# A two-layer transformer kernel on one core: the small transfers leave GpSimd's queue for SyncE's and ScalarE's

## The reference, cut to what matters

```
layer 1: h = rmsnorm(x);  z = h @ w_in           (pooling, q, k, v, and an index head that picks 64 keys)
         x = x + concat(pool_mixer(..), attention(..)) @ w_out
         x = x + conv_ffn(rmsnorm(x))            (w_up 2048 x 11264, causal 3-tap conv, silu(gate)*val, w_down)
layer 2: proj = rmsnorm(x) @ w_in_2              (rope attention "moba", latent attention "mla", two gates)
         mixed = g_a * (y_a @ w_branch_a) + g_b * (y_b @ w_branch_b)
         x = x + mixed @ w_out_2
         x = x + (silu(hn @ w_gate) * (hn @ w_up)) @ w_down,  hn = rmsnorm(x);  out = rmsnorm(x)
```

## Time and profile before

| | us |
|---|---|
| median of 3 runs | 2383.08 |
| the profiled execution, its time | 2383.49 |
| the profiled execution, its span | 2381.6 |
| PE busy in the span | 2365.1 |
| DVE busy | 1390.7 |
| ACT busy | 1194.4 |
| POOL busy | 128.8 |

### The profile page before, as it was taken

The page is one execution under the profiler, slowest core; times in us unless marked ns, Lnnn a source line. Parts: engine busy times, 40 slices in busy tenths (PEclk is TensorE's granted clock), DMA queues, the critical chain, the costliest instruction groups (busy, mean ns, idle before and its releaser), DMA issues.

```text
span 2381.6 us, 29812 instructions
## 1 busy us (share of the span) xinstructions
PE 2365.1 (99%) x10624; PEld 1958.6 (82%) x10624; DVE 1390.7 (58%) x1574; ACT 1194.4 (50%) x1489; POOL 128.8 (5%) x228
## 2 busy tenths in 40 slices
PE   9999999999999999999999999999999999999997
PEld 7788888888888888888888888888888888888886
DVE  6785465776766765555554554766555555555543
ACT  6455455666666544445455544555444444444442
POOL 0100010000000000002130000122000000000000
PEclk9999999999999999999999999999999999999999
DMA  8775467788787766666776556666777777776554
GB/s 303 194 206 173 146 224 211 217 225 216 205 226 219 207 215 202 203 203 195 202 193 198 162 164 186 210 219 215 211 201 200 210 202 210 202 200 221 194 194 136
DMA packets 443082, 483.52 MB, mean 203 GB/s; under 512 B 208000, under 2 KB 225808, under 8 KB 442864
## 3 DMA queue, kind: packets, MB, share of 16 engines
q1 hardware_dynamic: 437712, 474.83, 67.7%
q0 software_dynamic: 4704, 6.44, 1.0%
q10 hardware_dynamic: 576, 1.05, 0.1%
HBM read 448.12 MB, written 2.10 MB: 189 GB/s over the span
## 4 chain that ended last, share of the span: by engine, by line
PE 97%; SPq 1%; issue 0%; DMA 0%; ACT 0%; DVE 0%; POOLq 0%; POOL 0%; DVEq 0%; ACTq 0%
PE acc L727 31%; PE acc L729 31%; PE acc L728 31%; SPq L504 1%; PE pair_banks L898 1%; PE bank L718 0%; PE pair_banks L929 0%; PE acc L753 0%; PE acc L757 0%; PE acc L760 0%; DMA w_raw<-in_w_in 0%; PE pair_banks L959 0%; PE pair_banks L870 0%; PE pair_banks L930 0%; SPq L373 0%
## 5 line engine op out<-in xcount | busy, mean ns | idle before, releaser
L1430 DVE TENSOR_TENSOR w_lo<-w_raw,w_hi 128x1024 fp32r<-128x1024 f32 (+1 forms) x842 | 1024.7, 1220 | 928.3 <-ACT w_hi L1068 926.7
L1068 ACT ACTIVATE w_hi<-w_raw 128x1024 fp32r<-128x1024 f32 (+1 forms) x842 | 886.2, 1055 | 1051.4 <-PE acc L729 1003.3
L727 PE MATMUL acc<-w_hi,xT 128*128 128x512 f32 (+1 forms) x2208 | 862.7, 391 | 0.0
L729 PE MATMUL acc<-w_hi,xT 128*128 128x512 f32 (+1 forms) x2208 | 857.1, 388 | 0.0
L728 PE MATMUL acc<-w_lo,xT 128*128 128x512 f32 (+1 forms) x2208 | 856.6, 388 | 0.0
L727 PEld LDWEIGHTS acc<-w_hi,xT 128*128 128x128 f32 x2208 | 414.6, 188 | 86.9 <-issue 2.3
L729 PEld LDWEIGHTS acc<-w_hi,xT 128*128 128x128 f32 x2208 | 414.5, 188 | 85.7
L728 PEld LDWEIGHTS acc<-w_lo,xT 128*128 128x128 f32 x2208 | 414.7, 188 | 83.5
L727 PE MATMUL acc<-w_hi,f_hi 128*128 128x512 f32 x688 | 267.6, 389 | 0.0
L728 PE MATMUL acc<-w_lo,f_hi 128*128 128x512 f32 x688 | 267.6, 389 | 0.0
L729 PE MATMUL acc<-w_hi,f_lo 128*128 128x512 f32 x688 | 267.6, 389 | 0.0
(11 more groups left out here) (220 smaller groups left out, 1308.4 us busy)
## 6 DMA issues: line engine op xcount, KB each, us to landing
w_raw<-in_w_up SPq DMA_DIRECT2D x264, 512.0 KB, 4.2
w_raw<-in_w_in SPq DMA_DIRECT2D x198, 512.0 KB, 3.8
w_raw<-in_w_down SPq DMA_DIRECT2D x176, 512.0 KB, 4.6
w_raw<-in_w_gate SPq DMA_DIRECT2D x88, 512.0 KB, 3.6
w_raw<-in_w_out SPq DMA_DIRECT2D x64, 512.0 KB, 4.6
w_raw<-in_w_branch_a SPq DMA_DIRECT2D x16, 512.0 KB, 4.2
w_raw<-in_w_branch_b SPq DMA_DIRECT2D x16, 512.0 KB, 4.8
halves<-stage SPq DMA_DIRECT2D x208, 32.0 KB, 2.6
```

The costliest lines, as they stand in the source:

```text
L727: pe.matmul(o, l, w_hi[:, slot, k, 0:width], start=start, stop=False)
L729: last = pe.matmul(o, m, w_hi[:, slot, k, 0:width], start=False, stop=stop)
L1068: act.activation(in_slot(w_hi, slot, width), in_slot(w_raw, slot, width), ACT.Copy).then_inc(w_split_hi, 1)
L1430: dve.tensor_tensor(in_slot(w_lo, slot, width), in_slot(w_raw, slot, width), in_slot(w_hi, slot, width).bitcast(F32), ALU.subtract).then_i ...
```

## The change

POOL issues no transfers. For n = 0, 1 and 2 of the residual groups and of the mix, SP issues all 16 transfers, four at each of the steps b to b+3, and the split (`split_x`, `split_mix`) moves from step b+3 to b+7. For n = 3 SP issues eight at step b as before and ScalarE the other eight at step b, and the split stays at b+3. The five loads of constants are issued by SP after the loads of chunks 19 to 23, that of pool_w by SP at its own step. The move steps of the units qn 1, qr and qa 1 come 2, 4 and 4 steps later, and `copy_k` of ka 2 steps later.

```diff
         put(n + lead, "blocks", u, g)
+        later = {("qn", 1): 2, ("qr", 2): 4, ("qa", 1): 4}.get((name, half), 0)
         for b in range(4):
-            put(n + lead + b, "move", u, g, b)
+            put(n + lead + later + b, "move", u, g, b)
         if name in ("k1", "ka"):
-            put(n + lead + 6, "copy_k", u, g)
+            put(n + lead + (6 if name == "k1" else 8), "copy_k", u, g)
...
-            put(b, "move_x", 0)
-            put(b, "move_x", 1)
-            put(b + 3, "split_x", n, gain)
+            for part in range(4) if n < 3 else (None,):
+                put(b + (part or 0), "move_x", n + 4 * quarters, part)
+            put(b + (7 if n < 3 else 3), "split_x", n, gain)
...
+    put(b + 19, "load_pool")
...
-        put(b, "move_mix", 0); put(b, "move_mix", 1); put(b + 3, "split_mix", n)
+        for part in range(4) if n < 3 else (None,):
+            put(b + (part or 0), "move_mix", n, part)
+        put(b + (7 if n < 3 else 3), "split_mix", n)
...
+        def move_blocks_of(queue, part, first_half, to, from_, done):
+
+            for k in range(4) if part is not None else range(8):
+                b, a_ = (part, k) if part is not None else (k // 2, k % 2 + (0 if first_half else 2))
+                move_block(queue, to, from_, b, a_).then_inc(done, 16)
+
+        def move_x(queue, n, part, first_half):
+
+            queue.wait_ge(x_blocks, NT * (n + 1))
+            move_blocks_of(queue, part, first_half, flat_stage[1], flat_stage[0], x_moved)
...
                 if not chunk.per:
+                    if 20 <= chunk.now < 25:
+                        load_constant(chunk.now - 20)
...
+                        elif step_ == "load_pool":
+
+                            sp.wait_ge(rel_full, 6)
+                            sp.dma_start(pool_w[:], a["pool_w"].rearrange("w (k p) d -> p w k d", p=P)).then_inc(pool_loaded, 16)
...
-            def on_move_x(half):
-                if half == 1:
-                    move_x(pool, x_moves, 1)
...
+            def on_move_x(n, part):
+                if part is None:
+                    move_x(act, n, part, False)
+
+            def on_move_mix(n, part):
+                if part is None:
+                    move_mix(act, n, part, False)
+
             def on_split_x(n, gain):
                 n_x[0] += 1
-                for half in range(2):
-                    act.wait_ge(x_moved[half], 16 * 8 * n_x[0])
+                act.wait_ge(x_moved, 256 * n_x[0])
```

More of the change, by code:

```diff
@@ L104, in attend, with residual @@
         put(a + 7, "split_y", which, pair)
-    def residual(n, g, b, gain):
+    def residual(n, g, b, gain, quarters=None):
         put(b, "res", g, n)
@@ L146, in plan @@
         b = group("w_out", CW * n, CW, [0, 1, 4, 5, 6, 7, 2, 3] if n == 0 else whole, "y")
-        residual(n, len(groups) - 1, b, G_FFN1)
+        residual(n, len(groups) - 1, b, G_FFN1, 0)
     up1 = b
@@ L154, in plan @@
         b = group("w_down", CW * n, CW, list(range(FT // KC)), "f")
-        residual(n, len(groups) - 1, b, G_ATTN2)
+        residual(n, len(groups) - 1, b, G_ATTN2, 1)
     b = group("w_in_2", 3072, 512, whole, "x")
@@ L191, in plan @@
         put(b, "mix_b", n, len(groups) - 1)
-        put(b, "move_mix", 0); put(b, "move_mix", 1); put(b + 3, "split_mix", n)
+        for part in range(4) if n < 3 else (None,):
+            put(b + (part or 0), "move_mix", n, part)
+        put(b + (7 if n < 3 else 3), "split_mix", n)
     for n in range(4):
         b = group("w_out_2", CW * n, CW, whole, "m")
-        residual(n, len(groups) - 1, b, G_FFN2)
+        residual(n, len(groups) - 1, b, G_FFN2, 2)
     up2 = b
@@ L356, in two_layer_kernel @@
         unit_blocks, unit_moved, k_copied = sem("unit_blocks"), [sem(f"unit_moved{k}") for k in range(4)], sem("k_copied")
-        mix_blocks, mix_moved = sem("mix_blocks"), [sem("mix_moved_sp"), sem("mix_moved_pool")]
+        mix_blocks, mix_moved = sem("mix_blocks"), sem("mix_moved")
         mix_high, mix_low = sem("mix_high"), sem("mix_low")
         x_blocks, x_high, x_low = sem("x_blocks"), sem("x_high"), sem("x_low")
-        x_moved = [sem("x_moved_sp"), sem("x_moved_pool")]
+        x_moved = sem("x_moved")
         dve_step, pool_step, normalised = sem("dve_step"), sem("pool_step"), sem("normalised")
@@ L373, in move_block, with move_mix @@
             return queue.dma_start(dst, src)
[L375 to L389, removed]
+        def move_blocks_of(queue, part, first_half, to, from_, done):
[5 more added lines that the diff above has]
+            move_blocks_of(queue, part, first_half, flat_stage[1], flat_stage[0], x_moved)
+        def move_mix(queue, n, part, first_half):
+            queue.wait_ge(mix_blocks, n + 1)
+            move_blocks_of(queue, part, first_half, flat_half, flat_stage[1], mix_moved)
         def turned(unit, q):
@@ L453, in _ @@
         def _(sp):
-            chunk, products, x_moves, mix_moves = Count(), Count(), [0, 0], [0, 0]
+            chunk, products = Count(), Count()
             def load_x(n):
@@ L482, in load, with load_constant @@
                 if not chunk.per:
+                    if 20 <= chunk.now < 25:
+                        load_constant(chunk.now - 20)
                     for step_, *args in at.get(chunk.now - RING - LEAD - 1, []):
[L484 to L487, removed]
+                        if step_ == "move_x":
+                            move_x(sp, *args, True)
+                        elif step_ == "move_mix":
+                            move_mix(sp, *args, True)
+                        elif step_ == "load_pool":
+                            sp.wait_ge(rel_full, 6)
+                            sp.dma_start(pool_w[:], a["pool_w"].rearrange("w (k p) d -> p w k d", p=P)).then_inc(pool_loaded, 16)
                         elif step_ == "move":
                             move_unit(*args)
+            def load_constant(k):
+                if k == 0:
+                    sp.dma_start(cols[:, CONV_COL:], a["columns"][:, CONV_COL:]).then_inc(taps_loaded, 16)
+                elif k == 1:
+                    sp.dma_start(causal[:], a["c_causal"]).then_inc(const_loaded, 16)
+                elif k == 2:
+                    sp.dma_start(pool_m[:], a["c_pool"]).then_inc(const_loaded, 16)
+                elif k == 3:
+                    sp.dma_start(cos[:, 0, :], a["c_freq"]).then_inc(const_loaded, 16)
+                else:
+                    sp.dma_start(pos_i[:], a["positions_2"][0, :].rearrange("(t p) -> p t", p=P),
+                                 allow_slow_non_contiguous=True).then_inc(const_loaded, 16)
             def move_unit(u, g, b):
@@ L594, in _ @@
         def _(pool):
[L597 to L607, removed]
+            n_rstd, n_heads, n_roped, n_lat, steps = [0], [0], [0], [0], [0]
             def step(ins):
@@ L627, in on_rstd @@
                 n_rstd[0] += 1
-                if n_rstd[0] == 1:
-                    load_constants()
-            def on_move_x(half):
-                if half == 1:
-                    move_x(pool, x_moves, 1)
-            def on_move_mix(half):
-                if half == 1:
-                    move_mix(pool, mix_moves, 1)
             def on_lat(kind):
@@ L683, in on_rope @@
                 pool.sem_inc(roped, 1)
-            mine = {"headsq": on_heads, "rstd": on_rstd, "rstd0": on_rstd, "lat_rstd": on_lat, "rope": on_rope,
-                    "move_x": on_move_x, "move_mix": on_move_mix}
+            mine = {"headsq": on_heads, "rstd": on_rstd, "rstd0": on_rstd, "lat_rstd": on_lat, "rope": on_rope}
             for n in range(n_end + 8):
                 for step_, *args in at.get(n, []):
-                    if step_ == "isc" and args[0] == 5:
-                        pool.wait_ge(rel_full, 6)
-                        pool.dma_start(pool_w[:], a["pool_w"].rearrange("w (k p) d -> p w k d", p=P)).then_inc(pool_loaded, 16)
                     if step_ in mine:
@@ L1218, in on_split_mix @@
             def on_split_mix(n):
-                for half in range(2):
-                    act.wait_ge(mix_moved[half], 16 * 8 * (n + 1))
+                act.wait_ge(mix_moved, 256 * (n + 1))
                 for q in range(4):
@@ L1266, in _ @@
                     "copy_p": on_copy_p, "copy_d": on_copy_d, "copy_kr": on_copy_kr, "copy_kn": on_copy_kn,
-                    "split_y": on_split_y, "split_x": on_split_x, "split_pool": on_split_pool,
+                    "split_y": on_split_y, "split_x": on_split_x, "move_x": on_move_x, "move_mix": on_move_mix, "split_pool": on_split_pool,
                     "split_lat": on_split_lat, "split_mix": on_split_mix, "square": on_square,
```

## The result

The changed kernel takes 2393.68 us (median of 5 runs, 2392.98 to 2395.88) against 2383.08 us before (2382.54 to 2383.52): slower by 10.6 us, a ratio of 1.0048 (95% interval 1.0035 to 1.0060). I had forecast 2383.8 and a range of 2378 to 2391.

The account below looks back on a forecast made before the run. TensorE was taken as busy nearly throughout, leaving the hole near 1184 to 1216 us, the tail and the group boundaries. -5.4 - 2.1 + 4.55 + 3.7 = +0.75 on 2383.08 gave 2383.8 us, range 2378 to 2391.

Parts of the forecast that it names:

- part 5: SP's added issues for n = 0 to 2 and the constants: delay hidden by ScalarE's three-chunk lead, cost nothing.
- part 4: ScalarE's eight issues for n = 3, 5.1 us a burst, make chunk b+4 late at four places: 3.7 us lost.
- the sum: Whole kernel: -5.4 - 2.1 + 4.55 + 3.7 = +0.75 us, no change that can be told.
- Part 1: Program's end: with no transfers issued by POOL its DRAIN is short, so the span ends 5.4 us earlier.
- Part 2: TensorE's three waits near 1184 to 1216 us: spreading the transfers and moving copy_k gains 2.1 us.
- Part 3: Split of n = 2 at b+7: stops before the next matrix, 1.6 (w_out), 1.6 (w_out_2), 1.35 (mix); 4.55 us.
- My sign of being wrong: ScalarE's row of eight issues for n = 3: under 4 or over 6 us would show the prediction wrong.
- rival B: ScalarE's n = 3 issues cost more beside SP's, sharing one generator; decides from 6.1 us a burst, 2404 at 10.2; chance 0.17.
- A: Program's end: POOL's DRAIN stays long, since powers also ran between the two DRAINs; +6.15, 2389.2 us, slower; chance 0.18.
- C: ScalarE's burst for n = 3 is cheap, 3.5 us like its own loads; sum -2.9, 2380.2 us; chance 0.17.
- D: Neither the b+7 split nor ScalarE's issues cost, the step order being misjudged; -7.5, 2375.6 us, faster; chance 0.1.
- E: Hole near 1184 to 1216 us: five issues in 3.2 us still lag, 2.1 not gained; 2385.9 us; chance 0.08.

Follow-up runs that it names:

- experiment 10: The kernel before, only with the later move steps of qn 1, qr and qa 1 and the later copy_k of ka: 2380.43 us, ratio 0.9989.
- experiment 9: The kernel before, only with the splits of n = 0 to 2 of x and mix at b+7: 2388.01 us, ratio 1.0020.
- experiment 7: The changed kernel with the splits of n = 0 to 2 at b+6 instead of b+7: 2398.28 us, ratio 1.0065.
- experiment 1: The changed kernel with POOL instead of ScalarE issuing the second eight transfers for n = 3: 2386.15 us, ratio 1.0014.
- experiment 8: The changed kernel with the mix as before (eight each on SP and POOL at step b, split at b+3): 2385.10 us, ratio 1.0011.
- experiment 5: The changed kernel with POOL taking SP's eight transfers for n = 3, ScalarE still issuing its eight: 2391.75 us, ratio 1.0037.
- experiment 6: The changed kernel with the 16 transfers of n = 3 dealt 12 to SP and 4 to ScalarE: 2387.18 us, ratio 1.0017.
- experiment 3: The changed kernel with one transfer, the load of pool_w, back on POOL: 2396.33 us, ratio 1.0055.
- experiment 4: The changed kernel with the move steps of qn 1, qr, qa 1 and copy_k where they were before: 2397.35 us, ratio 1.0060.

## Why the prediction was wrong

Three steps failed: part 5, which put SP's delay at nothing, for the mix (3.4 us of stop); part 4, whose burst of 5.1 us measured 5.42 to 6.92 (2.5 us); and the sum, which has no term for matmuls at half pace behind a stop (4.8 us).

**Part 1, the tail: right in size (5.4), incomplete in cause.** I took the DRAIN for a matter of yes or no. The experiments give 0.644 us with no transfer of POOL, 0.752 with 1, 3.287 with 32, 5.247 with 56, 5.898 with 64 and 11.125 with 134: 0.64 and 0.08 for each. It is their number, and not what they move: one load of 1 MB adds 0.108 us, 32 transfers that move 1 MB together add 2.64. So POOL could have kept about 60 for nothing, and the change paid to move these as well.

**Part 2, the hole: right.** 2.1 forecast, 2.3 in the trace; 2.7 between the medians of experiment 10.

**Part 3, the split at b+7: right for x, wrong for the mix.** 1.54 twice for 1.6. At the mix the step that failed is in part 5: I let ScalarE's lead of three chunks hide SP's delay of 0.5 us a chunk, for x and mix alike, and then, in part 3, reckoned with a ScalarE that is on time. The lead does hide a late split from TensorE's chunks; it does not hide it from a step that stands behind that split and has its own deadline. The rows had a difference that I did not weigh: for n = 3, SP's transfers start 4.8 us after ScalarE's split of chunk b+3 at w_out and 6.2 us after it at the mix. In the changed kernel the delay also feeds on itself there: the weights come late (ahead of its split at 1542.36 ScalarE stood 2.66 us for them), so ScalarE and VectorE are late with their splits, so the turned blocks are late too, and SP starts the transfers of n = 2 only 9.0 us after TensorE's chunk b began; in experiment 9 it was 6.5. The step alone costs 1.30 (experiment 9); the stop stays at 4.38 with the step one earlier and SP as full (experiment 7), and at 5.04 without ScalarE's bursts (experiment 1); it is gone with SP relieved and the step back (experiment 8).

**Part 4, ScalarE's burst: mechanism right, size wrong.** It took 6.92, 6.32 and 6.49 us at w_down, the mix and w_out_2 and 5.42 at w_out, where I had 5.1 from SP's row at w_out; SP's own row at w_down, 5.58, would have given 2.1 instead of 1.6 us there. My sign of being wrong, a row over 6 us, came in three places of four, and so did rival B's bound of 6.1. But B's reason, SP issuing beside it, is only about half of it: without SP the four bursts are still 5.27 to 6.00. At the mix the longer burst cost little (0.52 us for 1.7), because the stop of 4.76 ahead of it had moved the need by that much. By the rule of the Trainium skill's page "Perfetto Trace Analysis" (section "DMA Instruction — HWDGE (DVE, Sync)"), that the generator is locked for each issue, 16 issues should have taken turns; SP's eight in 5.96 and ScalarE's in 6.92 at the same time (the rows of w_down after) do not take turns for their whole length, and experiment 5 puts SP's part at 0.15 to 0.9 us. At w_in_2 the burst's length sets the stop one for one (experiments 5 and 6), and without the burst no stop is left at any chunk 4 (experiment 1).

**What no step had: the clock.** A stop of 3.5 or 4.8 us can cost more than its length. Behind these two, 7 and 14 matmuls ran at half pace, 4.35 us in the profile. The medians differ by 9.9 us more than I had forecast. The profile has 3.4 of it at the mix's chunk 0, 2.5 in part 4 (6.18 for 3.7) and 4.8 in slow matmuls; less 0.1 of part 3 at x, 0.2 of part 2 and the 1.05 of the start that is 9.3.

The rivals A, C, D and E did not happen. Of the chance of slower, 0.33, about half was A's, for a cause that was not there, and half B's, whose cause is half the burst's excess and none of the mix's stop. No rival had the cause that costs most.

## What to carry to other kernels

- An engine that runs ahead hides a delay only from work whose deadline it is ahead of. When a step is moved towards its deadline, work out the engine's lateness at that very step, with everything queued ahead of it, in each stage by itself.
- Before a cost is removed entirely, see what sets it: here POOL's share of the tail grew with the number of its transfers and was hidden up to about 60. The version that keeps 64 on the idle queue, and with them the early splits, is 18 us below the one that moves all.
- Issues on an engine that computes are not free: eight cost ScalarE 5.3 to 7.1 us over all runs, all in front of its next work.

## What the runs showed of the hardware that I had not expected

- POOL's DRAIN at the end: 0.64 us and about 0.08 for each of its transfers (0.083 at 32 and 0.082 at 64, 0.078 at 134; six counts, nine traces with at least one). In experiments 1 and 3 the last of them had been issued over 700 and over 2200 us before. What the queue does in that time no trace shows.
- The half pace behind a stop is not the same each time: behind stops of 3.5 to 3.7 us at w_in_2 it lasted 7 matmuls in the changed kernel, 14 in experiment 3, and 1 in experiments 4 and 8, so it cost 0.1 to 2.9 us. Whether this is what scatters the times is not shown: five executions of the changed kernel span 2.9 us (2392.98 to 2395.88), six of the version without any such stop 2.1 (2374.68 to 2376.80).
